# RWKV-7 chunk stage of a two-layer decoder step: the second eight heads' 16-token level moved into the first half of a chunk

## The chip, the core and the metric

The kernel runs on one core of a Trainium2 chip. A core has five engines that run their own instruction streams and meet at semaphores: TensorE (PE, matrix products; PEld is its weight load), VectorE (DVE), ScalarE (ACT), GpSimd (POOL) and SyncE (SP), which issues most DMAs. The metric is the device time of one execution in microseconds (us); the median of 3 runs before the change is 3222.52 us (3216.25 to 3230.39).

## The reference

Two layers over a prompt (1024 tokens and 16 meta tokens) and eight samples of 4 tokens: layer 0 mixes tokens with latent attention, layer 1 with RWKV-7 time mixing; each is followed by a squared-ReLU MLP. The change lies in RWKV-7's recurrence, cut here to what it computes for each of 16 heads of 64 channels:

```python
def _wkv_step(S, inp):
    r, w, k, v, a, b = inp
    sa = jnp.einsum('bhvk,bhk->bhv', S, a)
    S = S * w[:, :, None, :] + sa[..., None] * b[:, :, None, :] + v[..., None] * k[:, :, None, :]
    return S, jnp.einsum('bhvk,bhk->bhv', S, r)

S_T, y = lax.scan(_wkv_step, wkv0, (tm(r), tm(decay), tm(k), tm(v), tm(-kk), tm(kk * a)))
```

Here r, k, v are projections of the token-shifted input, decay = exp(-exp(log_w)), kk the normed key and a a learned rate. y then goes through a group norm over each head, gets a bonus term, is multiplied with a gate g and projected.

## The kernel before

The recurrence is computed in chunks of 128 tokens: chunks 0 to 7 for the prompt, and a tail of 48 tokens (the last 16 tokens of the prompt and the samples). Within a chunk, sa of all tokens is the solution of a triangular system, (1 + M) sa = first sums, where M holds the products of decayed keys with b-keys below the diagonal. The kernel builds the inverse of the 128x128 triangle of each head level by level. VectorE makes the inverses of the 16x16 blocks on the diagonal (`low_inverses`, L4047), for the next chunk, at the end of each chunk. From them TensorE makes the larger ones: level 16 joins pairs of 16-blocks to 32-blocks, level 32 to 64-blocks, level 64 to the full 128. Each level is two products with a copy between: the *crossed* product of M with the smaller inverses, which VectorE (level 16, L4038, with a mask) or ScalarE (levels 32 and 64) copies negated out of PSUM, and the *joined* product, which gives the new off-diagonal block. ScalarE prepares the operand of a crossed product by spreading blocks: `spread_16` (L3062, 2 instructions of L3054) fills X4 from XE, `spread_32` (L3069) fills X5 (2 of L3054) and the diagonal of XT (4 of L3048) from what VectorE's `blocks_32` (L4041: add L4043, transpose L4045) made of level 16's result. Level 64 (L1529) first transposes blocks (L693), which ScalarE copies to XW6 (`take_turned`), then does its two products; the copies between are `take_w_64` (L3092) and `take_x_64` (L3096).

The sixteen heads are worked on in two halves of eight, d = 0 and d = 1. A half runs: masks of the products of keys (VectorE, L4007), level 16, 32, 64, `first_sums`, `finals` (sa, the state's product, the output's product). Between these steps the same loops prepare chunk c + 1 and finish chunk c - 1: `rates`, `decays` (L2997 to L3001), running sums (L3953), `a_keys` and `b_keys` (decayed keys on VectorE, L3936 and L3989), `key_factors` (ScalarE, eight instructions, L3103), `before_half` (TensorE's products of b-keys with the decayed keys, the M of the next chunk, masked by VectorE, L4007), `diagonals` (ScalarE, L3011, what `low_inverses` reads), and for the chunk before its centring, norm (POOL, L2375 to L2379), gates (TensorE) and their product (VectorE, L4140).

What sets the order: the code is written once for each engine (`chunk` appears in the streams of TensorE, ScalarE, VectorE and GpSimd), and each engine runs it strictly as written. PSUM is used as two rings of four banks, `ra` (drained by ScalarE) and `rv` (drained by VectorE): a product waits until the bank's last content was copied out, and the copies take the banks in the order in which TensorE filled them. `keep_busy` (L1440) is an empty product of 128x256, whose result nobody reads.

Of the kernel before, what the change touches and what calls it, by code (L numbers as in the profile page):

```python
# [216 lines left out]
def program(nc, A, O):  # L217
    ctx = ExitStack()
    with ctx:
# [457 lines left out]
        def _(pe):  # L677
# [815 lines left out]

            def level_16(c, d, ma, filler):

                apart(x4_b.sem, c * x4_b.per + d + 1)
                b = narrow(rv, rv.filled.n - 3)
                for j in range(8):
                    for rows, cols in diagonal(8 * d + j):
                        ins = mm(b[rows, j * 64:(j + 1) * 64], ma[rows, cols], X4[rows, j * 64:(j + 1) * 64], True, True)  # L1500
                rv.done(ins)
                w4_at = rv.filled.n
                filler()
                if d == 1:
                    keep_busy(rv)
                b = narrow(rv, w4_at)
                for j in range(8):
                    h = 8 * d + j
                    for rows, _ in diagonal(h):
                        ins = mm(b[rows, j * 32:(j + 1) * 32], W4[rows, j * 64:(j + 1) * 64], XD[rows, h * 32:(h + 1) * 32], True, True)  # L1510
                rv.done(ins)
# [19 lines left out]
            def level_64(d, ma, fillers):  # L1531

                crossed_at = ra.filled.n
                fillers[2]()
                keep_busy(ra)
                b = narrow(ra, crossed_at)
                for j in range(8):
                    ins = turn(b[0:64, j * 64:(j + 1) * 64], XT[0:64, j * P:j * P + 64], 64)
                ra.done(ins)
                turned_at = ra.filled.n  # L1540
                fillers[0]()
                keep_busy(ra)
                b = narrow(ra, turned_at)
                for j in range(8):
                    h = 8 * d + j
                    ins = mm(b[64:P, j * 64:(j + 1) * 64], ma[0:64, h * P + 64:(h + 1) * P], XW6[0:64, j * 64:(j + 1) * 64], True, True)
                ra.done(ins)
                w6_at = ra.filled.n
                fillers[1]()
                b = narrow(ra, w6_at)  # L1550
                for j in range(8):
                    ins = mm(b[0:64, j * 64:(j + 1) * 64], XW6[64:P, j * 64:(j + 1) * 64], XT[64:P, j * P + 64:(j + 1) * P], True, True)
                ra.done(ins)

            def chunk(c, par, nth, finish=True, prepare=True, wn=P):
# [14 lines left out]

                def finals(d, taken, stated):

                    keep_busy(ra)
                    ra.wait_drained()
# [37 lines left out]
                k_with_both(0, 1, ar)  # L1612
                level_16(c, 0, ma, lambda: turn_b_k(c, P))
                bonus_sums(c, P)
# [4 lines left out]
                v_in[par].wait(pe, nth)  # L1619
                level_64(0, ma, [when(prepare, lambda: key_sums(c + 1, wn)), lambda: first_sums(0), nothing])  # L1620
                finals(0, when(prepare, lambda: rates(c + 1, wn, 0)), when(prepare, lambda: (rates(c + 1, wn, 1), key_scales(c + 1, wn))))

                b_with_r(1, ar)
                k_with_both(1, 0, ar)
                k_with_both(1, 1, ar)
                level_16(c, 1, ma, nothing)
                if finish:
# [10 lines left out]

                level_32(c, 1, ma, when(prepare, lambda: before(0)))
                level_64(1, ma, [nothing, lambda: first_sums(1), when(prepare, lambda: before(1))])  # L1640
                finals(1, when(finish, lambda: turn_z(c - 1, P, Y[1 - par])), nothing)

# [810 lines left out]
        def _(act):  # L2453
# [608 lines left out]
            def spread_16(c, d):  # L3062

                low_b.wait(act, c)
                if not isinstance(c, int) or c > 0 or d > 0:
                    e32_b.wait(act, c, d)
                signal(pair_blocks(X4, XE[:, d * 256:(d + 1) * 256]), x4_b)
# [63 lines left out]
            def chunk(c, par, finish=True, prepare=True, wn=P):  # L3131
                if prepare:
                    lora_columns(c + 1, wn)
                tokens(P)
                bonus_out(P)
                spread_32(c, 0)
# [16 lines left out]
                if prepare:  # L3153
                    both_rates(c + 1, wn)
                spread_16(c, 1)
                if prepare:
                    decays(c + 1, wn, wn == TAIL)
                take(Y[par][:, 0:512], P, 512)
                if wn == TAIL:
                    decays_before(c + 1, wn)  # L3160
                if prepare:
                    key_factors(c + 1, wn)

                spread_32(c, 1)
                take_w_32()
                take_x_32()
                take_turned()
# [125 lines left out]
        def _(dve):  # L3293
# [868 lines left out]
            def chunk(c, par, finish=True, prepare=True, wn=P):  # L4162
# [14 lines left out]
                if finish:  # L4177
                    centre(c - 1, P, Y[1 - par])
                if prepare:
                    clamp(c + 1, wn)  # L4180
# [4 lines left out]
                if finish:  # L4185
                    scale_outputs(c - 1, P, Y[1 - par])
                new_taken()
                new_summed(0)
# [6 lines left out]
                k_with_both(1)  # L4195
                level_16(1)
                if prepare:
                    a_keys(c + 1, 1 - par, wn)
                blocks_32(c, 1)
                if prepare:  # L4200
                    b_keys(c + 1, wn)
# [197 lines left out]
```

## Time and profile before

| what | value |
|---|---|
| median of 3 runs | 3222.52 us |
| profiled execution | 3217.26 us, of them 3215.5 us span |
| granted TensorE clock, mean | 0.991 |
| busy, share of the span | PE 96%, PEld 89%, DVE 58%, ACT 42%, POOL 39% |
| chunk stage | chunk 0 starts at 1800.45 us, the tail's first products at 2330.65 us |
| chunk 3 (2002.83 to 2069.30, 66.47 us), busy us | PE 61.17, DVE 51.06, ACT 39.05, POOL 18.34, clock 1.00 |
| chunk 7 | crossed product of level 16, second half, starts at 2304.86 us; its eight key factors take 2.64 us |

How to read it: a row of a timeline gives the start in us from the span's start, the length in us, engine, line, operation, what it writes and reads with their shapes, and in brackets how long the engine sat idle before it and which instruction ended the wait. Most tiles are pieces of one allocation, `arena`; so an instruction is best known by its line and shape. The timeline shows two records for each of the small products, so 16 products read x32. A product's length includes the end of the pipeline: the next may start some 0.07 us before it ends. PEclk is the granted clock as a share of 2.4 GHz.

### The profile page before, as it was taken

The page shows a single profiled execution, that of the slowest core. Times are in us where ns is not written, and L with a number is a line of the kernel's source. Part 1 is how long each engine was busy: PE and PEld are TensorE (multiplying, and loading weights), DVE is VectorE, ACT ScalarE, POOL GpSimd, SP SyncE. Part 2 cuts the span into 40 slices and gives each one's busy share as a digit, 9 for nine tenths or more (in the row PEclk, how much of TensorE's full clock was granted, in tenths as well). Part 3 has the DMA queues.
Part 4 walks back from the last instruction along what each step waited for, and adds up shares of the span by engine and source line. Part 5 has one row for each costly group of instructions (what it writes and reads, how often), then busy time and mean ns, then how long its engine had stood idle before and what let it go on. Part 6 is the DMA issues. An engine that isn't in the chain of part 4 may idle for free.

```text
span 3215.5 us, 70230 instructions
## 1 busy us (share of the span) xinstructions
PE 3085.3 (96%) x25828; PEld 2853.0 (89%) x25828; DVE 1880.4 (58%) x3193; ACT 1358.9 (42%) x2823; POOL 1261.7 (39%) x877
## 2 busy tenths in 40 slices
PE   8999999998999999999999999998999999999998
PEld 8788887798999999998899878787888899999998
DVE  5666663257444578864412577777735644457885
ACT  4344445424554433322223455656522455443332
POOL 0000000025766777732222122232224467677771
PEclk9999999999999999999999999999999999999999
DMA  3222225402544544431123201001151254554442
GB/s 116 61 79 74 74 60 179 151 13 80 160 158 158 176 148 144 138 103 56 61 81 117 75 21 47 28 28 34 42 174 37 84 161 153 158 175 148 148 134 78
DMA packets 307311, 330.49 MB, mean 103 GB/s; under 512 B 54366, under 2 KB 289809, under 8 KB 306994
## 3 DMA queue, kind: packets, MB, share of 16 engines
q1 hardware_dynamic: 301166, 308.54, 30.3%
q0 software_dynamic: 5904, 19.21, 1.9%
q8 instruction: 133, 2.18, 0.3%
q14 instruction: 56, 0.46, 0.0%
q10 hardware_dynamic: 52, 0.10, 0.0%
HBM read 232.05 MB, written 116.16 MB: 108 GB/s over the span
## 4 chain that ended last, share of the span: by engine, by line
PE 74%; DVE 10%; PEld 5%; POOL 3%; ACT 3%; issue 2%; DMA 1%; PEldq 0%; DVEq 0%; SPq 0%; ACTq 0%; POOLq 0%
PE bank L685 70%; PEld bank L685 5%; PE bank L693 4%; DVE arena L3936 1%; DVE hT L4007 1%; POOL wloA L2215 1%; POOL arena L2215 1%; DVE arena L3600 1%; DVE x_mix L3890 1%; POOL wloS L2215 1%; DMA arena<-in_mla_w_qkv_a 1%; DVE arena L3311 1%; DVE arena L3471 1%; DVE arena L3953 0%; DVE x_lo L3897 0%
## 5 line engine op out<-in xcount | busy, mean ns | idle before, releaser
L685 PE MATMUL bank<-arena 64*128 64x128 f32 (+19 forms) x6718 | 770.7, 303 | 33.9 <-DVE hT L4007 12.9
L685 PEld LDWEIGHTS bank<-arena 128*128 128x128 f32 (+9 forms) x6718 | 602.5, 162 | 168.2 <-issue 35.1
L2462 ACT COPY arena<-bank 128x512 f32<-128x512 f32 (+14 forms) x518 | 230.6, 485 | 590.7 <-PE bank L685 390.0
L2741 ACT ACTIVATE whiS<-arena 128x512 fp32r<-128x512 f32 x180 | 112.9, 627 | 405.4 <-POOL arena L2215 392.1
L2215 POOL TENSOR_TENSOR wloA<-arena,whiA 128x512 fp32r<-128x512 f32 x180 | 263.5, 1478 | 14.0 <-ACT whiA L2735 14.0
L2215 POOL TENSOR_TENSOR wloS<-arena,whiS 128x512 fp32r<-128x512 f32 x180 | 241.1, 1353 | 49.1 <-ACT whiS L2741 49.1
L2215 POOL TENSOR_TENSOR arena<-arena 128x512 f32<-128x512 f32 x120 | 165.5, 1380 | 230.9 <-PE bank L685 230.9
L3805 DVE TENSOR_TENSOR hT<-hT,bank 128x536 f32<-128x536 f32 x280 | 197.4, 706 | 83.2 <-PE bank L685 82.9
L693 PE MATMUL bank<-table,arena 128*128 128x128 f32 (+5 forms) x1422 | 181.1, 269 | 28.2 <-DVE arena L3483 13.0
L3620 DVE TENSOR_TENSOR arena<-std,bank 128x268 f32<-128x268 f32 x192 | 80.4, 431 | 216.0 <-PE bank L685 208.2
L685 PE MATMUL bank<-hiT,whiS 128*128 128x268 f32 x768 | 199.9, 289 | 6.9 <-DVE fb L3615 3.5
L693 PEld LDWEIGHTS bank<-table,arena 128*128 128x128 f32 (+5 forms) x1422 | 146.2, 135 | 54.2 <-issue 40.7
L2185 POOL TENSOR_TENSOR arena<-arena 128x536 f32<-128x536 f32 (+3 forms) x18 | 39.2, 2177 | 330.2 <-ACT arena L2711 299.8
L3746 DVE TENSOR_TENSOR arena<-arena 128x268 f32<-128x268 f32 x224 | 140.7, 668 | 42.2 <-ACT arena L2779 39.9
L685 PEld LDWEIGHTS bank<-hiT,whiS 128*128 128x128 f32 x768 | 146.3, 191 | 8.0 <-DVE fb L3615 4.1
L3323 DVE TENSOR_TENSOR hT<-hT,bank 128x268 f32<-128x268 f32 (+2 forms) x120 | 55.1, 468 | 156.1 <-PE bank L685 155.7
L3890 DVE SCALAR_TENSOR_TENSOR x_mix<-arena,prm 128x384 f32<-128x384 f32 (+1 forms) x96 | 57.8, 674 | 149.5 <-PEq L1280 149.2
L685 PE MATMUL bank<-hi,whiA 128*128 128x268 f32 x512 | 132.6, 288 | 2.6 <-DVE fb L3615 1.7
L2208 POOL TENSOR_TENSOR q<-arena,q 64x1072 fp32r<-64x1072 f32 x4 | 9.8, 2459 | 316.4 <-ACT q L2603 316.4
L685 PE MATMUL bank<-loT,whiS 128*128 128x268 f32 x512 | 132.7, 288 | 0.0
L685 PE MATMUL bank<-fb,whiS 128*128 128x268 f32 x512 | 132.3, 288 | 0.0
L685 PE MATMUL bank<-fb,whiA 128*128 128x268 f32 x512 | 131.9, 287 | 0.0
(356 smaller groups left out, 8980.2 us busy)
## 6 DMA issues: line engine op xcount, KB each, us to landing
u_scratch<-arena SPq DMA_DIRECT2D x480, 134.0 KB, 1.8
arena<-in_ffn_w_up SPq DMA_DIRECT2D x64, 512.0 KB, 4.1
arena<-u_scratch SPq DMA_DIRECT2D x56, 536.0 KB, 5.1
arena<-in_ffn_w_down SPq DMA_DIRECT2D x112, 256.0 KB, 3.8
arena<-u_scratch SPq DMA_DIRECT2D x56, 402.0 KB, 5.8
arena<-past_scratch SPq DMA_DIRECT2D x32, 640.0 KB, 6.9
past_scratch<-in_cache_kv_latent SPq DMA_DIRECT2D x128, 128.0 KB, 2.4
past_scratch<-in_cache_k_rope SPq DMA_DIRECT2D x128, 32.0 KB, 2.1
```

What stands on the lines that cost most here:

```text
L685: return pe.matmul(out, lhsT, rhs, start=first, stop=last, skip_group_check=group)
L693: return pe.transpose(out, src, ident[0:rows, 0:rows])
L2185: lane.do(pool.tensor_tensor(sq[:, 0:n, :], sq[:, 0:n, :], sq[:, n:2 * n, :], ALU.add))
L2215: return pool.tensor_tensor(out, a, b, op)
L2462: lane.do(act.copy(dst, b if view is None else view(b)), ring.drained)
L2741: ins = act.activation(hi[name][:, :, :], src, ACT.Copy)
L3311: ins = dve.scalar_tensor_tensor(out=dst[:, k, at:at + w], in0=src[:, k, at:at + w], scalar=prm[:, k, row:row + 1], in1=by, op0=ALU.mult, ...
L3323: lane.do(dve.tensor_tensor(hT[:, k, at:at + w], hT[:, k, at:at + w], b[:, 0:w], ALU.add), ring.drained)
L3620: dve.tensor_tensor(out, to, (BV, BA)[s][CHAIN[i]][:, 0:TS], ALU.add).then_inc(to_dve_b[layer].sem, 1)
L3746: dve.tensor_tensor(f.us[q, s], f.us[a, s], f.us[b, s], op).then_inc(diff_b[layer].sem, 1)
L3805: ins = dve.tensor_tensor(to[i], to[i], made, ALU.add)
L3890: ins = dve.scalar_tensor_tensor(out=x_mix[:, k, at:at + w], in0=DX[:, k, at:at + w], scalar=prm[:, k, R_MU + row:R_MU + row + 1], in1=nT[ ...
```

## The change

The crossed product of level 16 of the second eight heads moves from the second half to the first, where it stands for an empty product before the transposes of level 64; the joined product stands for the empty product before `finals`. With them move VectorE's mask, the add and transpose of the 32-blocks, and ScalarE's `spread_16`, now ahead of the bonus copy. ScalarE's `spread_32` of the second half is put where `spread_16` stood, ahead of `decays`; the two copies of level 32 go ahead of `key_factors`. In the second half the products with the decayed keys of the next chunk (`before`) move from level 32 and level 64 into level 64 alone, in the place of two empty products. Per chunk five empty products go.

```diff
-            def level_16(c, d, ma, filler):
+            def crossed_16(c, d, ma):
...
-                w4_at = rv.filled.n
-                filler()
-                if d == 1:
-                    keep_busy(rv)
-                b = narrow(rv, w4_at)
+                mark["crossed_16", c, d] = rv.filled.n
+
+            def joined_16(c, d):
+
+                b = narrow(rv, mark["crossed_16", c, d])
...
                 crossed_at = ra.filled.n
                 fillers[2]()
-                keep_busy(ra)
                 b = narrow(ra, crossed_at)
...
                 fillers[0]()
-                keep_busy(ra)
+                if d == 0:
+                    keep_busy(ra)
...
-                def finals(d, taken, stated):
-
-                    keep_busy(ra)
+                def finals(d, hidden, taken, stated):
+
+                    hidden()
...
-                level_16(c, 0, ma, lambda: turn_b_k(c, P))
+                crossed_16(c, 0, ma)
+                turn_b_k(c, P)
+                joined_16(c, 0)
...
-                level_64(0, ma, [when(prepare, lambda: key_sums(c + 1, wn)), lambda: first_sums(0), nothing])
-                finals(0, when(prepare, lambda: rates(c + 1, wn, 0)), when(prepare, lambda: (rates(c + 1, wn, 1), key_scales(c + 1, wn))))
+                level_64(0, ma, [when(prepare, lambda: key_sums(c + 1, wn)), lambda: first_sums(0), lambda: crossed_16(c, 1, ma)])
+                finals(0, lambda: joined_16(c, 1), when(prepare, lambda: rates(c + 1, wn, 0)),
+                       when(prepare, lambda: (rates(c + 1, wn, 1), key_scales(c + 1, wn))))
...
-                level_16(c, 1, ma, nothing)
...
-                level_32(c, 1, ma, when(prepare, lambda: before(0)))
-                level_64(1, ma, [nothing, lambda: first_sums(1), when(prepare, lambda: before(1))])
-                finals(1, when(finish, lambda: turn_z(c - 1, P, Y[1 - par])), nothing)
+                level_32(c, 1, ma, nothing)
+                level_64(1, ma, [when(prepare, lambda: before(1)), lambda: first_sums(1), when(prepare, lambda: before(0))])
+                finals(1, lambda: keep_busy(ra), when(finish, lambda: turn_z(c - 1, P, Y[1 - par])), nothing)
```

ScalarE and VectorE (`spread_16` now waits for the mask after the crossed product that last read X4):

```diff
                 tokens(P)
+                spread_16(c, 1)
                 bonus_out(P)
                 spread_32(c, 0)
...
-                spread_16(c, 1)
+                spread_32(c, 1)
                 if prepare:
                     decays(c + 1, wn, wn == TAIL)
                 take(Y[par][:, 0:512], P, 512)
...
+                take_w_32()
+                take_x_32()
                 if prepare:
                     key_factors(c + 1, wn)
-
-                spread_32(c, 1)
-                take_w_32()
-                take_x_32()
                 take_turned()
...
                     centre(c - 1, P, Y[1 - par])
+                level_16(1)
...
                     scale_outputs(c - 1, P, Y[1 - par])
+                xt_b.wait(dve, c, 1)
+                blocks_32(c, 1)
                 new_taken()
...
-                level_16(1)
                 if prepare:
                     a_keys(c + 1, 1 - par, wn)
-                blocks_32(c, 1)
```

**TensorE, second half of chunk 3, before.** `64x64 x16` is a crossed product, `64x32 x16` level 16's joined product, `table 128x256` an empty product, `128x512` and `128x256 x2` the gates, `128x128 x8` a half of the products with the next chunk's decayed keys; the order counts each product once.

```order
L685 MATMUL bank<-arena,hT 64x64 x16
L685 MATMUL bank<-table 128x256
L685 MATMUL bank<-arena,hT 64x32 x16
L685 MATMUL bank<-arena 128x512
L685 MATMUL bank<-arena 128x256 x2
L685 MATMUL bank<-hT 64x64 x16
L685 MATMUL bank<-arena 128x128 x8
L685 MATMUL bank<-table 128x256
L685 MATMUL bank<-arena,hT 64x64 x16
L685 MATMUL bank<-arena 128x128 x8
L685 MATMUL bank<-table 128x256
L693 MATMUL bank<-table,arena 64x64 x8
```

The same place of the changed kernel:

```order
L685 MATMUL bank<-arena 128x256 x8
L685 MATMUL bank<-arena 128x512
L685 MATMUL bank<-arena 128x256 x2
L685 MATMUL bank<-hT 64x64 x16
L685 MATMUL bank<-table 128x256
L685 MATMUL bank<-arena,hT 64x64 x16
L685 MATMUL bank<-arena 128x128 x8
L693 MATMUL bank<-table,arena 64x64 x8
L685 MATMUL bank<-arena 128x128 x8
L685 MATMUL bank<-arena,hT 64x64 x8
L685 MATMUL bank<-arena 128x128 x4
```

The first rows (level 16 and an empty product) are gone, the gates follow the keys' products (`128x256 x8`) at once, and both halves of the decayed keys' products stand around the transposes (L693).

**ScalarE, the same half, before,** from `spread_16` (L3054 arena) on; L2997 to L3001 are the decays, L3103 the key factors, L3054 hT with L3048 `spread_32`, L3078 and L3084 the copies of level 32, `64x512` the copy of the transposed blocks.

```order
L3054 ACTIVATE arena<-arena,table 128x8x32 x2
L2997 ACT_TABLE_LOAD
L2997 ACTIVATE arena<-arena 128x1024
L2999 ACTIVATE arena<-arena 128x8
L3000 ACTIVATE arena<-arena 128x8
L3001 ACTIVATE arena<-arena 128x1024
L2462 COPY arena<-bank 128x512
L3103 ACTIVATE arena<-arena,prm 128x128 x8
L3054 ACTIVATE hT<-arena,table 128x8x32 x2
L3048 COPY arena<-arena 32x8x32 x4
L3078 ACTIVATE hT<-bank 32x8x32 x2
L3084 COPY arena<-bank 32x8x32 x2
```

And of the changed kernel, whose lines stand 2 to 4 further down:

```order
L3056 ACTIVATE hT<-arena,table 128x8x32 x2
L3050 COPY arena<-arena 32x8x32 x4
L2999 ACT_TABLE_LOAD
L2999 ACTIVATE arena<-arena 128x1024
L3001 ACTIVATE arena<-arena 128x8
L3002 ACTIVATE arena<-arena 128x8
L3003 ACTIVATE arena<-arena 128x1024
L2464 COPY arena<-bank 128x512
L3082 ACTIVATE hT<-bank 32x8x32 x2
L3088 COPY arena<-bank 32x8x32 x2
L3107 ACTIVATE arena<-arena,prm 128x128 x8
L2464 COPY arena<-bank 64x512
```

`spread_32` now stands ahead of the decays, and the key factors between the second copy of level 32 and the copy of the transposed blocks.

**VectorE, end of the first half of the changed kernel:** L4124 is the centring, L4041 the mask of level 16, L4046 and L4048 the add and transpose of the 32-blocks, L4154 the state update.

```order
L4124 TENSOR_TENSOR arena<-arena 128x1024
L4041 TENSOR_TENSOR hT<-bank,arena 128x512
L3943 TENSOR_SCALAR arena<-bank 128x128
L4128 TENSOR_REDUCE arena<-arena 128x16
L3965 RECIPROCAL arena<-arena 128x128
L4133 RECIPROCAL arena<-arena 128x16
L4135 TENSOR_TENSOR arena<-arena 128x1024
L4046 TENSOR_TENSOR arena<-arena,bank 128x256
L4048 STREAM_TRANSPOSE arena<-arena 128x256
L4154 TENSOR_TENSOR arena<-bank,table 128x512
L3939 TENSOR_TENSOR arena<-arena 128x512 x2
```

In the kernel before, L4041, L4046 and L4048 (there L4038, L4043 and L4045) are not in this piece; they stand in the second half around the decayed keys (L3936).

## Rows read from the trace of the kernel before

**Rows 1.** Timeline of TensorE, chunk 3: start, length, line, tiles, [idle before].
```profile
2012.07 1.15 PE L685 MATMUL bank<-hT 64*64 64x64 f32 x32 [1.09 <-ACT hT L3054]
...
2016.30 0.60 PE L693 MATMUL bank<-table,arena 64*64 64x64 f32 x8 [0.29 <-ACT arena L3084]
...
2023.12 0.70 PE L685 MATMUL bank<-table 128*128 128x256 f32 x2
...
2041.79 1.12 PE L685 MATMUL bank<-arena,hT 64*64 64x32 f32 x32 [0.36 <-DVE hT L4038]
2042.84 1.99 PE L685 MATMUL bank<-arena 128*128 128x512 f32 x6
2045.22 1.15 PE L685 MATMUL bank<-hT 64*64 64x64 f32 x32 [0.39 <-ACT hT L3054]
2047.38 1.16 PE L685 MATMUL bank<-arena 64*128 64x128 f32 x16 [1.01 <-DVE arena L4140]
...
2053.29 1.11 PE L685 MATMUL bank<-arena,hT 64*64 64x64 f32 x16
...
2057.16 1.14 PE L685 MATMUL bank<-arena 64*64 64x64 f32 x16
```

**Rows 2.** Timeline of VectorE, chunks 2 and 3.
```profile
1989.30 1.06 DVE L4059 STREAM_TRANSPOSE arena<-arena 128x512 f32<-128x512 f32 x1 [0.49 <-ACTq L3013]
...
2002.83 3.80 DVE L4007 TENSOR_TENSOR hT<-bank,arena 128x512 f32<-128x512 f32 x6 [1.09 <-PE bank L685]
...
2029.69 2.79 DVE L3936 TENSOR_TENSOR arena<-arena 128x512 f32<-128x512 f32 x2
...
2040.96 0.68 DVE L4038 TENSOR_TENSOR hT<-bank,arena 128x512 f32<-128x512 f32 x1
2041.75 1.43 DVE L3936 TENSOR_TENSOR arena<-arena 128x1016 f32<-128x1016 f32 x2
...
2044.08 1.22 DVE L3936 TENSOR_TENSOR arena<-arena 128x1024 f32<-128x1024 f32 x1
...
2051.37 1.29 DVE L4007 TENSOR_TENSOR arena<-bank,arena 128x512 f32<-128x512 f32 x2 [1.54 <-PE bank L685]
...
2055.77 1.05 DVE L4059 STREAM_TRANSPOSE arena<-arena 128x512 f32<-128x512 f32 x1 [0.49 <-ACTq L3013]
```

**Rows 3.** Timeline of ScalarE, chunk 3.
```profile
2009.98 0.27 ACT L2462 COPY arena<-bank 128x128 f32<-128x128 f32 x1 [0.91 <-PE bank L685]
2010.86 0.91 ACT L3054 ACTIVATE hT<-arena,table 128x256 f32<-128x256 f32 x2 [0.61 <-DVE arena L4045]
...
2032.62 0.91 ACT L3054 ACTIVATE arena<-arena,table 128x256 f32<-128x256 f32 x2 [0.17 <-issue]
...
2037.37 1.06 ACT L2997 ACTIVATE arena<-arena 128x1024 f32<-128x1024 f32 x1 [2.55 <-DVE arena L3957]
...
2039.95 3.19 ACT L3103 ACTIVATE arena<-arena,prm 128x128 f32<-128x128 f32 x8
...
2044.83 1.63 ACT L3048 COPY arena<-arena 32x256 f32<-32x256 f32 x4
...
2052.57 0.58 ACT L2462 COPY arena<-bank 64x512 f32<-64x512 f32 x1 [1.54 <-PE bank L693]
2053.17 2.55 ACT L3011 ACTIVATE arena<-arena 32x512 f32<-32x512 f32 x4
```

**Rows 4.** Timeline of GpSimd, chunk 3.
```profile
2028.84 2.36 POOL L2379 TENSOR_TENSOR arena<-arena 128x1024 f32<-128x1024 f32 x1
...
2039.65 2.37 POOL L2351 TENSOR_TENSOR arena<-arena 128x1024 f32<-128x1024 f32 x1 [8.45 <-ACT arena L3001]
```

**Rows 5.** Timeline of TensorE, chunk 7.
```profile
2315.89 1.11 PE L685 MATMUL bank<-arena,hT 64*64 64x64 f32 x16
```

**Rows 6.** TensorE in chunk 0.
```profile
1810.86 0.64 PE L685 MATMUL bank<-arena 128*32 128x128 f32 x16 [2.09 <-ACT arena L2462]
```

**Rows 7.** Windows, chunk 0: length, busy PE, PEld, DVE, ACT, POOL; PEclk, DMA, GB/s.
```profile
1812.00:1814.00 2.00, 1.54 (x13) 0.84 (x13) 0.00 (x0) 1.98 (x7) 0.00 (x0) 0.50 1.00 354
```

More of the change, by code:

```diff
@@ L3064, in spread_16 @@
                 low_b.wait(act, c)
-                if not isinstance(c, int) or c > 0 or d > 0:
-                    e32_b.wait(act, c, d)
+                if d == 1:
+                    act.wait_ge(v_drained, mark["crossed_16", c, 0])
+                elif c > 0:
+                    act.wait_ge(v_drained, mark["crossed_16", c - 1, 1])
                 signal(pair_blocks(X4, XE[:, d * 256:(d + 1) * 256]), x4_b)
@@ L4195, in chunk @@
                 k_with_both(1)
-                level_16(1)
                 if prepare:
                     a_keys(c + 1, 1 - par, wn)
-                blocks_32(c, 1)
-                if prepare:
                     b_keys(c + 1, wn)
```

## The prediction

> **What bounds the kernel now.** I went from the page to the windows view, then read one chunk of the stage engine by engine in the timelines. The page has TensorE busy for 96% of the span, so a gain must come from TensorE's waits or from work taken off it. The changed code runs only in the eight chunks of the mixing stage (1800 to 2333 us of 3215.5). A steady chunk repeats every 66.47 us (2055.77 less 1989.30, [rows 2]); TensorE is busy for 61.2 of it at full clock (table above). Its 5.3 us of waits lie where four 16-to-64-token levels follow one another. In the second half the order reads: crossed product of level 16, which ends at 2040.7, an empty product, a wait of 0.36 us for VectorE, joined product, gates, a wait of 0.39 for ScalarE's spread, crossed product of level 32, a wait of 1.01 until VectorE has made the keys of the next chunk, and only at 2053.29 the first product of the last level [rows 1]. From there TensorE runs without a wait to the end of the chunk, so what the change does to that start, and to the third product of the level (2057.16), is what it does to the chunk. VectorE is the next candidate: at the chunk's start it waits 1.09 us for TensorE [rows 2], and by no more than that may it fall behind TensorE.
>
> I number times as in chunk 3, whose first mask starts at 2002.83.
>
> **First half: what is added.** ScalarE spreads the second eight heads' blocks ahead of the bonus copy: 0.91 us and 0.17 of issue (2032.62, [rows 3]). Ahead of the bonus copy and of spread_32 it idles 0.91 and 0.61 us [rows 3]; 1.08 fits into 1.52, so spread_32 still starts at 2010.86. The crossed product (1.15 us) takes the place of an empty one (0.63 to 0.70) before the transposes at 2016.30, where TensorE waits 0.29 for ScalarE anyway [rows 1]; it ends at 2016.4, 0.1 late. The next two steps wait for ScalarE's copies, which swallow that. VectorE's mask for it (0.68) falls into an idle stretch. The joined product (1.12, of which 1.05 until the next may start) takes the place of the empty one of 0.70 at 2023.12, where nothing waits: TensorE is 0.35 us late from there on. VectorE's add and transpose come then, and it has nothing else until the state's product at 2029.
>
> Is 0.35 us paid? VectorE's state update starts at 2029.69 and its two adds take 2.79 us, where the same two take 1.42 elsewhere; GpSimd's add runs from 2028.84 to 2031.20 [rows 2, 4]. I read the 1.37 us as VectorE standing still until GpSimd is done. Its end does not move with 0.35 us, so VectorE's chain to the masks at 2037.26 and their end at 2040.96 stay where they are. Price in a steady chunk: 0. Bounds: 0 and 0.35.
>
> The Trainium skill has this as a rule ("SBUF — State Buffer", section "Who interferes with whom"): a VectorE instruction with two SBUF inputs and a GpSimd instruction that reads SBUF use one read interface, and the second to issue blocks until the first is done. The trace agrees (1.37 us).
>
> **Second half: what goes.** TensorE has both products of level 16 behind it. After the keys' masks the gates can start where the crossed product stood, at 2041.79 - 0.36 - 0.70 - 1.08 = 2039.65; they take 2.0 us (the banks they need are drained by the third to fifth of the six masks, in time), so level 32's crossed product starts at 2041.65 and no longer at 2045.22. ScalarE has spread its operand long before: spread_32 now stands where the 0.91 us of spread_16 stood, and is longer by its four copies, 1.63 us. Behind it ScalarE waits 2.55 us for the running sums of the decays (2037.37, [rows 3]); that cover takes all of it in a steady chunk, with 0.9 left.
>
> From the crossed product to ScalarE's last copy of level 32 it takes 2016.30 - 0.14 - 2012.07 = 4.09 us in the first half [rows 1], so here until 2045.75. And now the edit that costs: the eight key factors (3.19 us, 2039.95, [rows 3]) ran in ScalarE's gap before level 32; they now stand between it and the copy of the transposed blocks. ScalarE is done with them at 2048.95, copies until 2049.55 (0.58), and TensorE's first product of the last level starts at 2049.7: 3.6 us earlier than 2053.29.
>
> Meanwhile VectorE: masks end at 2040.96, the level-16 mask (0.68) is gone. The decayed keys can be issued at 2041.05. But GpSimd's product runs from 2039.65 to 2042.02 [rows 4], and both read two SBUF tiles: by what 2029.69 showed the keys wait, and end at 2043.2, where they end now (2041.75 + 1.43). The add and transpose of level 32 are gone too, so b_keys start at 2043.2 where they started at 2044.08: 0.9 earlier. The product with the decayed keys follows b_keys' start by 2047.38 - 2044.08 = 3.3 us, so it starts at 2046.5. TensorE has waited from 2044.8, 1.7 us, its longest wait of the chunk. Then 1.1 of product, 0.55 of transposes, the second product at 2048.15, done at 2049.3; the masks of it 2049.35 to 2050.65 (1.29, [rows 2]); ScalarE's diagonals 2.55 us to 2053.25; only behind them its copy for the third product, 0.6, so that product starts at 2054.05. By TensorE's own pace (2057.16 - 2053.29 = 3.87) it would be 2053.55. The later counts: 2057.16 - 2054.05 = **3.1 us a steady chunk**.
>
> VectorE's inverses start with the diagonals at 2053.3 and not at 2055.77: 2.45 earlier, TensorE 3.1. The 0.65 us between them fit into VectorE's 1.09 [rows 2].
>
> **The sum.** Chunks 1 to 6: 6 x 3.1 = 18.6. Chunk 0: TensorE waits for ScalarE there (2.09 us at 1810.86, [rows 6]), so the 1.08 us of spread_16 are paid, and without an earlier chunk's output GpSimd has no add that hides the 0.35: 3.1 - 1.4 = 1.7, of which I take 1.6, since spread_32 has less cover there. Chunk 7: its crossed product started at 2304.86; the gates take that place, 0.35 late, and the first product of the last level follows at 2305.2 + 2.0 + 4.1 + 2.64 (shorter key factors) + 0.7 = 2314.7, against 2315.89 [rows 5]: 1.2. In all **21.4 us**. The profiled execution took 3217.3 us, so it would be 3195.9; the median of the runs is 3222.5, 5 us higher, and that is what I start from: 3222.5 - 21.4 = **3201 us**. Everything behind the stage hangs on it in a chain and moves with it.
>
> **Bounds.** Of what no row shows: the keys blocked by GpSimd (end 2043.2) or not (2042.4); the longest wait of TensorE (1.7 us) without a price or with one; the 0.35 us. Per steady chunk that makes 3.6 at best, 1.2 at worst; I take 3.1, since the one row that shows such an overlap (2029.69) shows the full block.
>
> **Rivals.**
> *VectorE sets the end.* If its inverses begin later than I say, or its slack of 1.09 is less than it looks, TensorE waits at the next chunk's first masks and the gain is VectorE's, 2.45: 6 x 2.45 + 2.8 = 17.5, 3205 us. For it: just 0.45 us of slack would be left. Against: each step of it was read from rows.
> *No block of the keys.* They end 0.8 earlier, everything behind b_keys too, and TensorE's own pace and the key factors decide: 3.6, so 6 x 3.6 + 2.8 = 24.4, 3198 us. For it: the rows cannot show who would wait. By the page's rule above the block comes, since GpSimd starts first.
> *The clock falls once a chunk.* Five empty products of 0.63 us go, and a wait of 1.7 us comes. In chunk 0, after a wait of 2.09 us, the granted clock was 0.50, which is 1.2 GHz, from 1812 to 1814 [rows 6, 7], and it was back at full only near 1816. Some 3.8 us at half speed cost up to 1.9 us; in seven chunks 13, so 3222.5 - 21.4 + 13 = 3214 us. Against: waits of 1.0 to 1.1 us, three a chunk, leave the clock at 1.00 now.
> *Slower: the clock stays down.* The same mechanism, longer: from 2049.7 TensorE works without a pause, and each microsecond of it at 1.2 GHz costs half. From 6.2 us at half speed a chunk (3.1 / 0.5) the gain is gone; 12 us cost 6.0 - 3.1 = 2.9 a chunk, 20 in seven: 3243 us. Against: in chunk 0 the clock was back after dense work.
>
> **Chances.** Forecast 0.52 (3196 to 3207 by itself), VectorE 0.15, no block 0.12, clock once a chunk 0.17, clock for long 0.04. A change of this kernel can be told from none from about 0.5%, 16 us. Below 3206 lie nearly all of the first and third and over half of the second: faster 0.70; within 0.5% 0.26; slower 0.04. Range 3193 to 3214.
>
> **What would show it.** The period of the diagonals' transpose on VectorE should be 63.4 us (66.47 before). TensorE's wait ahead of the decayed keys' product should be 1.7 us, and the keys on VectorE 2.1 us from issue where GpSimd overlaps. ScalarE should have no idle time between the last copy of level 32, the key factors and the copy of the transposed blocks. VectorE's wait at a chunk's first mask should shrink from 1.09 to about 0.45; at 0 with TensorE waiting there, the first rival holds. A granted clock below 1.00 in chunks 1 to 7 speaks for the third. A period above 65 us would make the forecast wrong.

## The result

The changed kernel takes 3229.16 us (median of 20 runs, 3218.71 to 3240.49) where the kernel before takes 3222.84 us (20 runs, 3215.61 to 3230.39): the ratio is 1.0025, 95% interval 1.0015 to 1.0034. It is slower by a quarter of a percent; 3201 was forecast. Its profiled execution took 3219.73 us, one of its shorter ones: the profile below shows some 9 us less of the loss than the median run has.

The page of the profile after, its first lines and the clock:

```profile
span 3217.9 us, 70070 instructions
PE 3077.1 (96%) x25748; PEld 2861.2 (89%) x25748; DVE 1889.7 (59%) x3193; ACT 1359.4 (42%) x2823; POOL 1263.1 (39%) x877
...
PEclk9999999999999999999999989999889999999999
```

With five empty products a chunk gone, TensorE is busy for 57.2 us in a chunk with full clock and no longer for 61.2. Over the whole kernel its busy time fell by 8 us only: the rest went into products that took longer. The mean granted clock fell from 0.991 to 0.983, and three slices of the chunk stage and the tail (the 24th, 29th and 30th of 40) show an eight where there were nines.

The windows view of the changed kernel, four stretches: columns as in the rows of before, with the busy us of each engine and PEclk third from the end.

```profile
core 0: us, PE busy (x) PEld busy (x) DVE busy (x) ACT busy (x) POOL busy (x), PEclk, DMA share, GB/s
1998.58:2061.76 63.18, 57.22 (x749) 50.45 (x749) 52.47 (x88) 39.06 (x85) 18.33 (x9) 1.00 0.10 35
1919.00:1937.00 18.00, 18.00 (x114) 17.18 (x111) 16.19 (x41) 7.35 (x14) 0.00 (x0) 0.53 0.09 30
2308.00:2326.00 18.00, 16.27 (x89) 15.71 (x90) 12.82 (x38) 6.03 (x13) 1.86 (x3) 0.53 0.42 79
2346.00:2364.00 18.00, 18.00 (x253) 15.20 (x250) 3.85 (x7) 2.01 (x4) 8.89 (x4) 0.53 0.40 139
```

Two kinds of chunk show. The first row is a chunk from one diagonals' transpose to the next with the clock at 1.00: it takes 63.18 us, where before it took 66.47 [rows 2]. The second row is the last level of chunk 1: TensorE has no wait at all and a clock of 0.53, that is nearly all of it at the lower of the two levels, 1.2 GHz. I call such a stretch at 1.2 GHz a spell. Read in steps of one microsecond from 1780 to 2380 us, the spells of the changed kernel add up to 65 us: 3.4 and 3.4 in chunk 0, 3.4 and 17.1 in chunk 1, 3.4 in chunk 2, 17.1 in chunk 7 and 17.1 in the tail. Those of the kernel before add up to 17 (3.4 in chunk 0 and 13.7 in the tail). The difference of 48 us at half speed is 24 us of time. The forecast's gain of 21.4 less those 24 leaves a loss of 2.6, and the two spans differ by 2.4.

The table gives the periods of VectorE's transpose that opens `low_inverses`, from the one for chunk n to the one for chunk n + 1 (each is made at the end of the chunk ahead of its own, so the spell from 1919 to 1937 lies in both the second and the third column):

| kernel | 0 to 1 | 1 to 2 | 2 to 3 | 3 to 4 | 4 to 5 | 5 to 6 | 6 to 7 | 7 to tail |
|---|---|---|---|---|---|---|---|---|
| before | 71.18 | 66.47 | 66.46 | 66.47 | 66.47 | 66.47 | 66.46 | 61.71 |
| after | 69.70 | 69.30 | 73.33 | 63.18 | 63.19 | 63.17 | 63.18 | 59.29 |

From the first to the last of them after is 7.4 us shorter (524.3 against 531.7); behind the last, where chunk 7's last level and the tail each ran some 18 us at 0.53, it is 8.7 longer, and ahead of the first 1.1. That makes the 2.4 us by which the spans differ.

TensorE in a chunk with full clock (chunk 3 of the changed kernel), second half:

```profile
2047.25 3.05 PE L685 MATMUL bank<-arena 64*128 64x256 f32 x14 [1.11 <-DVE hT L4010]
...
2052.34 1.15 PE L685 MATMUL bank<-arena,hT 64*64 64x64 f32 x32 [0.33 <-ACT hT L3082]
2055.23 1.16 PE L685 MATMUL bank<-arena 64*128 64x128 f32 x16 [1.74 <-DVE arena L4143]
...
2058.22 1.11 PE L685 MATMUL bank<-arena,hT 64*64 64x64 f32 x16 [0.48 <-ACT arena L2464]
...
2062.54 1.11 PE L685 MATMUL bank<-arena 64*64 64x64 f32 x16 [0.38 <-ACT arena L3096]
```

The wait ahead of the product with the decayed keys is 1.74 us where it was 1.01 [rows 1], the last level starts at 2058.22, 0.48 us after TensorE was ready, and its third product waits 0.38. The wait of 1.74 us alone does not always bring a fall: in this execution it stands in chunks 2 to 6 and the clock stayed at 1.00 behind it each time. The falls came behind waits of 1.60 (chunk 0), 2.09 (chunk 1) and 2.19 us (chunk 7), and in the first halves of chunks 0 to 2 behind 1.67 to 4.27 us. And the same place in chunk 1, where the clock fell:

```profile
1917.97 1.16 PE L685 MATMUL bank<-arena 64*128 64x128 f32 x16 [2.09 <-DVE arena L4143]
...
1919.38 1.86 PE L685 MATMUL bank<-arena 64*128 64x128 f32 x15
1921.17 1.96 PE L685 MATMUL bank<-arena,hT 64*64 64x64 f32 x16
1923.07 2.07 PE L685 MATMUL bank<-arena 128*128 128x128 f32 x8
1924.93 3.51 PE L685 MATMUL bank<-std,hT 128*128 128x64 f32 x16
1928.38 1.97 PE L685 MATMUL bank<-arena 64*64 64x64 f32 x16
```

Here the wait was 2.09 us, and from 1919 on each product takes nearly twice its length: 1.96 for 1.11, 2.07 for 1.16, 3.51 for 1.90. That lasts until 1937, through work without a gap.

The other engines in the chunk with full clock, VectorE, then ScalarE, then GpSimd:

```profile
2011.49 3.80 DVE L4010 TENSOR_TENSOR hT<-bank,arena 128x512 f32<-128x512 f32 x6 [0.46 <-PE bank L685]
...
2049.81 3.34 DVE L3939 TENSOR_TENSOR arena<-arena 128x1016 f32<-128x1016 f32 x3
```

```profile
2046.03 1.06 ACT L2999 ACTIVATE arena<-arena 128x1024 f32<-128x1024 f32 x1 [1.06 <-DVE arena L3960]
...
2054.28 3.19 ACT L3107 ACTIVATE arena<-arena,prm 128x128 f32<-128x128 f32 x8
2057.50 0.58 ACT L2464 COPY arena<-bank 64x512 f32<-64x512 f32 x1
2059.15 2.55 ACT L3013 ACTIVATE arena<-arena 32x512 f32<-32x512 f32 x4 [1.07 <-DVEq L4017]
```

```profile
2048.31 2.36 POOL L2353 TENSOR_TENSOR arena<-arena 128x1024 f32<-128x1024 f32 x1 [8.45 <-ACT arena L3003]
```

VectorE's first wait is 0.46 us (1.09 before, [rows 2]); its three key instructions take 3.34 us, where the same three take 2.63 when GpSimd is out of the way (below); ScalarE had 1.06 us of cover left ahead of the decays (0.9 forecast) and runs from the key factors into the copy of the transposed blocks without a gap.

### The profile page after: what moved, and what is told of

Its sections match the earlier page's. It is cut to its first block, busy times and chain, and to the rows that moved or that the text cites. A ratio compares the mean times of both kernels' runs of the same rounds, so it can differ in the third digit from the quotient of the medians.

```text
span 3217.9 us, 70070 instructions
## 1 busy us (share of the span) xinstructions
PE 3077.1 (96%) x25748; PEld 2861.2 (89%) x25748; DVE 1889.7 (59%) x3193; ACT 1359.4 (42%) x2823; POOL 1263.1 (39%) x877
## 4 chain that ended last, share of the span: by engine, by line
PE 75%; DVE 10%; PEld 5%; ACT 3%; POOL 2%; issue 1%; DMA 1%; DVEq 1%; PEldq 0%; SPq 0%; ACTq 0%; POOLq 0%
PE bank L685 71%; PEld bank L685 5%; PE bank L693 4%; DVE arena L3939 1%; DVE hT L4010 1%; POOL wloA L2217 1%; DVE arena L3603 1%; POOL arena L2217 1%; POOL wloS L2217 1%; DVE x_mix L3893 1%; DMA arena<-in_mla_w_qkv_a 1%; DVE arena L3314 1%; DVE arena L3474 1%; DVE arena L3956 0%; DVE x_lo L3900 0%
## 5 line engine op out<-in xcount | busy, mean ns | idle before, releaser
L685 PE MATMUL bank<-arena 64*128 64x128 f32 (+19 forms) x6718 | 781.3, 306 | 42.5 <-DVE hT L4010 12.8
L685 PEld LDWEIGHTS bank<-arena 128*128 128x128 f32 (+9 forms) x6718 | 614.6, 165 | 173.0 <-issue 39.9
L693 PE MATMUL bank<-table,arena 128*128 128x128 f32 (+5 forms) x1422 | 183.7, 271 | 26.3 <-DVE arena L3486 13.1
L693 PEld LDWEIGHTS bank<-table,arena 128*128 128x128 f32 (+5 forms) x1422 | 148.6, 136 | 48.2 <-issue 33.8
L685 PE MATMUL bank<-arena,hT 64*64 64x64 f32 (+2 forms) x1920 | 126.6, 239 | 7.2 <-ACT hT L3082 3.5
L685 PEld LDWEIGHTS bank<-arena,hT 64*64 64x64 f32 (+1 forms) x1920 | 116.1, 155 | 18.7 <-issue 18.7
```

Source lines behind the costliest of these rows:

```text
L685: return pe.matmul(out, lhsT, rhs, start=first, stop=last, skip_group_check=group)
L693: return pe.transpose(out, src, ident[0:rows, 0:rows])
```

## The experiments

Each was run 4 to 12 times, beside the kernel before, whose median was then 3219.4 to 3220.6 us. The places are named by the second half of a chunk: the first place is the wait ahead of the product with the decayed keys, the second the wait ahead of the last level's first product.

**Is it the waits?** Two empty products into the 1.74 us wait:

```diff
-                level_64(1, ma, [when(prepare, lambda: before(1)), lambda: first_sums(1), when(prepare, lambda: before(0))])
+                level_64(1, ma, [when(prepare, lambda: before(1)), lambda: first_sums(1), when(prepare, lambda: ([keep_busy(ra) for _ in range(2)], before(0)))])
```

> The changed kernel with two empty products (2 x 0.63 us) put into its wait of 1.74 us ahead of the product with the decayed keys. Theory (the lost time is TensorE's clock, which falls in that wait and keeps the last level at half speed): steady chunks keep their 63.2 us, the clock stays at 1.00 in chunks 1 to 6, no spell at half speed begins at that place; time 3199 us (0.993 of before). Rival A (the spells begin somewhere else, the wait only happens to be near): spells as in the changed kernel, time 3225 to 3235. Rival B (the empty products themselves cost): period 63.2 + 1.3 = 64.5, time near 3210. In chunk 0 and chunk 7 the wait ahead of the last level (1.6 and 2.2 us) is left, so a spell there may remain.

Measured: 0.9952 of the kernel before (0.9935 to 0.997), 3209.7 us, with spells at half speed in chunks 0, 1, 2 and 7 in the profiled execution (its slowest, 3221.8) and a period of 63.16 to 63.6 in the others. Half-way: right in kind, but 10 us short of the theory's 3199. The clock fell in chunks 1 and 2 as well, where the theory had none: in chunk 1 from 1928 on, behind the last level's third product and its wait of 0.73 us, in chunk 2 in the first half, behind a wait of 2.69.

The same with one more empty product after the second product with the decayed keys (`lambda: (before(1), keep_busy(ra))`):

> As the run before, with one more empty product between the second product with the decayed keys and the last level's first product (a wait of 0.48 us in steady chunks, 1.6 in chunk 0, 2.2 in chunk 7). Theory: no spell of half speed in any chunk except perhaps the first half of chunk 0; period 63.2 to 63.3 us, because the third product of the last level is released by ScalarE's diagonals, not by this; time 3197 us. Rival A: no better than the changed kernel, 3225 to 3235. Rival B: 0.1 to 0.2 us more per chunk than the run before.

Measured: **0.9934** (0.9918 to 0.995), 3200.2 us, runs within 3198.6 to 3204.3. TensorE in this kernel, chunk 3:

```profile
2038.49 1.13 PE L685 MATMUL bank<-table 128*128 128x256 f32 x4
2040.31 1.16 PE L685 MATMUL bank<-arena 64*128 64x128 f32 x16 [0.69 <-DVE arena L4143]
```

```profile
2042.76 0.70 PE L685 MATMUL bank<-table 128*128 128x256 f32 x2
2043.38 1.14 PE L685 MATMUL bank<-arena,hT 64*64 64x64 f32 x16
```

The two empty products fill 1.13 us, the wait left is 0.69; the third stands where 0.48 us of wait was. The period is 63.2 us (64.0 and 63.5 in two chunks), and no spell at half speed is left ahead of the tail's. TensorE does more work than in the changed kernel (58.86 us busy in a chunk, 57.22 there) and the kernel is 29 us faster. This is the forecast's 3201 us; the theory had 3197.

**Count or place?** Three empty products a chunk as well, but ahead of `finals` of the second half, where TensorE does not wait (`lambda: keep_busy(ra)` becomes `lambda: [keep_busy(ra) for _ in range(4)]`):

> The changed kernel with three more empty products a chunk, as many as in the run with both places filled (0.9934 of before), but put where TensorE has no wait, ahead of finals of the second half. Theory (what counts is that the waits of the last level are filled): the clock falls as in the changed kernel, and 3 x 0.63 = 1.9 us a chunk are paid on top: period about 65.1 where the clock is full, 3235 to 3250 us. Rival (any empties hold the clock up, wherever they stand): clock at 1.00 in chunks 1 to 6, 3210 to 3215 us.

Measured: 1.0069 (1.0053 to 1.0084), 3238.8 us, half speed in chunks 0, 1, 2, 5, 6 and 7 (0.51 at 1988 to 1995, for one). Where the clock was full the period was 64.14 us, not 65.1: four empty products in a row take 1.99 us where one takes 0.70, so three more add 1.3 and not 1.9. The place decides.

**Order or empties?** The kernel before, in its own order, without the five empty products:

```diff
                 fillers[2]()
-                keep_busy(ra)
...
                 fillers[0]()
-                keep_busy(ra)
+                if d == 0:
+                    keep_busy(ra)
```

(and without the one in `level_16` for d = 1 and the one of `finals` for d = 0).

> The kernel before, in its own order, without the five empty products per chunk that the change took out. Theory: its waits become longer but stay below 1.7 us, so that spells at half speed are fewer than in the changed kernel or none; if the empties alone held the clock up, spells appear in chunks 1 to 7 here as well and the time is 3230 to 3245. If the reordering is what brings the fall (one wait of 1.74 us instead of three short ones), the time is 3218 to 3223, 0 to 0.5 us a chunk less than before, with the clock at 1.00 in chunks 1 to 6.

Measured: 1.0059 (1.0036 to 1.0081), 3240.2 us. Windows of this kernel around the last level of a first half (level 64 of the first eight heads, chunk 3), then one period of it:

```profile
core 0: us, PE busy (x) PEld busy (x) DVE busy (x) ACT busy (x) POOL busy (x), PEclk, DMA share, GB/s
2018.00:2023.00 5.00, 4.33 (x47) 4.13 (x45) 2.29 (x3) 3.17 (x6) 0.72 (x1) 1.00 0.01 3
2023.00:2031.00 8.00, 8.00 (x55) 7.43 (x56) 0.77 (x2) 4.05 (x10) 6.32 (x3) 0.57 0.00 0
1919.78:1987.91 68.13, 61.05 (x750) 53.67 (x748) 50.79 (x88) 39.02 (x85) 18.33 (x9) 0.95 0.10 32
```

The clock falls in chunk after chunk (0.57 from 2023 to 2031; 0.95 over a period, which is 68.13 and not 66.47 us long), and from chunk 1 to chunk 7 no wait of TensorE is longer than 1.2 us. But these falls lie in the *first* half, in chunks 1, 2, 3, 4, 6 and 7 (one more, of 3.4 us, begins in chunk 7's second half). TensorE in chunk 3, its first half and then its second:

```profile
2010.36 1.15 PE L685 MATMUL bank<-hT 64*64 64x64 f32 x32 [1.10 <-ACT hT L3053]
...
2014.54 0.60 PE L693 MATMUL bank<-table,arena 64*64 64x64 f32 x8 [0.87 <-issue]
...
2022.15 5.02 PE L685 MATMUL bank<-arena 128*128 128x64 f32 x34 [0.67 <-ACT arena L3095]
```

```profile
2042.61 1.12 PE L685 MATMUL bank<-arena,hT 64*64 64x32 f32 x32 [0.99 <-DVE hT L4037]
...
2048.08 1.16 PE L685 MATMUL bank<-arena 64*128 64x128 f32 x16 [1.01 <-DVE arena L4139]
...
2053.24 1.11 PE L685 MATMUL bank<-arena,hT 64*64 64x64 f32 x16 [0.76 <-ACT arena L2461]
```

In the first half the two waits of 0.87 and 0.67 us stand where the empty products were. The changed kernel has level 16's moved products in these two places, and behind them no fall begins in any chunk of its profile. In the second half three empty products are gone as well and the waits are 0.99, 1.01 and 0.76 us, and in the profiled execution no spell begins there in chunks 1 to 6. So two things follow. A long wait is not needed for a fall, and taking the empties out of the old order costs 20 us. But where the changed kernel loses its clock, in the second half, the removal alone did not bring the fall in this execution; what the new order adds there is the longer wait.

**One empty product, in one place or the other.** Only in the first (`range(1)`), only in the second:

> The changed kernel with one empty product, not two, in the first place and none in the second; 1.1 us of the wait of 1.74 are left. Theory: between the changed kernel and the run with two in the first place (0.9952 of before): 3210 to 3225 us. Rival (a single empty product is enough): 3200 to 3210 us.

> The changed kernel with one empty product in the second place alone (ahead of the last level's first product; waits of 0.48, 1.6 and 2.2 us in chunks 3, 0 and 7). Theory: the wait of 1.74 us is left, so the clock still falls in some chunks, less often than in the changed kernel: 3208 to 3225 us. Rival (the second wait alone is the cause): as good as with both places filled, 3198 to 3203 us.

Measured: 0.9988 (0.9977 to 1.0), 3216.9 us, runs from 3203 to 3222; and 0.9979 (0.9963 to 0.9996), 3213.2 us, runs from 3203 to 3239. Both lie where the theory had them. A profile alone would mislead: the one of the first shows no spell in chunks 1 to 6 (its execution took 3206), and six of its ten other runs took over 10 us more.

**Key factors early.** ScalarE's `key_factors` back ahead of `take_w_32()`:

> The changed kernel with ScalarE's eight key factors (3.19 us) put back ahead of its two copies of level 32. Theory: the last level's first product starts earlier (right behind the transposes' copy, some 0.5 us sooner), but its third product is released by the diagonals and stays: period 63.2 us, unchanged; the wait ahead of the last level goes (0.48, 1.6 and 2.2 us in chunks 3, 0 and 7), the wait of 1.74 us stays, so spells at half speed remain in some chunks but not in chunk 7: 3215 to 3230 us. Rival (key factors in the last level are what costs): period 62.7 or less and a time below 3205.

Measured: 1.0087 (1.0066 to 1.0107), 3249.6 us: 20 us above the theory's range. TensorE around one last level:

```profile
2118.10 1.15 PE L685 MATMUL bank<-arena,hT 64*64 64x64 f32 x32 [0.71 <-ACT hT L3082]
2120.62 1.16 PE L685 MATMUL bank<-arena 64*128 64x128 f32 x16 [1.36 <-DVE arena L4143]
```

```profile
2127.92 1.11 PE L685 MATMUL bank<-arena 64*64 64x64 f32 x16 [0.90 <-ACT arena L3096]
2128.97 0.95 PE L685 MATMUL bank<-table 128*128 128x256 f32 x2
2129.71 3.67 PE L685 MATMUL bank<-arena 128*128 128x64 f32 x16
2133.17 1.91 PE L693 MATMUL bank<-table,arena 128*128 128x128 f32 x8
```

The wait ahead of the last level's first product is gone, as expected. The other waits are 0.71, 1.36 and 0.90 us; in the changed kernel they were 0.33, 1.74, 0.48 and 0.38. So the longest is shorter, the last one, ahead of the third product, is longer, and the sum is the same (3.0 and 2.9 us). The clock falls around this place in each of the chunks 1 to 6, where the changed kernel's profile shows it in one of them. Chunk 7 has no spell in its last level, as expected. The spell brings a second one, in the next first half. VectorE, then GpSimd, then TensorE there:

```profile
2148.98 2.94 DVE L4003 TENSOR_TENSOR arena<-arena 128x1024 f32<-128x1024 f32 x1
```

```profile
2148.92 1.93 POOL L2348 TENSOR_TENSOR arena<-arena,prm 128x1024 f32<-128x1024 f32 x1 [5.47 <-DMA arena<-k_scratch]
```

```profile
2153.98 1.97 PE L685 MATMUL bank<-hT 64*64 64x64 f32 x32 [2.82 <-ACT hT L3056]
...
2157.14 3.36 PE L685 MATMUL bank<-arena,hT 64*64 64x64 f32 x64
```

Half speed held TensorE back, but not VectorE's inverses nor GpSimd, which so comes to its product (2148.92) just when VectorE scales the state: 2.94 us instead of 1.22. Behind it TensorE waits 2.82 us for the operand of level 32, and is slow again (1.97 for 1.15). The changed kernel has it too: waits of 2.69 and 4.27 us at 1882.02 and 1956.42, after the spells of chunks 0 and 1.

**Does that clash matter?** GpSimd's next keys only after the state is scaled (`s_b.wait(pool, c)` ahead of `scale_keys`):

> The changed kernel, in which GpSimd starts on the next chunk's keys only when VectorE has scaled the state. Theory (a spell at half speed in the last level holds TensorE back but not VectorE and GpSimd; in the next first half GpSimd's product then falls on VectorE's state update, and TensorE waits 2.7 to 4.3 us for the level-32 operand and slows again): the wait ahead of level 32 in the first half stays at 1.1 us in every chunk and no spell begins there; the first falls, in the wait of 1.74 us, stay: 3212 to 3226 us, below the changed kernel. Rival (the spells in the first half have nothing to do with GpSimd): waits of over 2.5 us ahead of level 32 remain, 3226 to 3236 us.

Measured: 1.0023 (1.0004 to 1.0042), 3229.2 us, the changed kernel's own time and above the theory's 3212 to 3226. The mechanism is as said: from chunk 1 on the wait ahead of level 32 is 1.1 us and no spell begins there. But the gain did not come. In the profiled execution (3247.4 us) the clock fell around the last level of nearly every chunk, with spells of up to 20.5 us. The clash follows from a spell; taking it away alone does not shorten the median.

**GpSimd's block of the decayed keys.** GpSimd's product of r after the b-keys (`b_b.wait(pool, c)` for `dec_b.wait(pool, c)` in `decay_r`):

> The changed kernel, in which GpSimd makes its product of r with the decays (2.36 us, now beside VectorE's decayed keys) only after VectorE's b-keys. Theory: VectorE's first decayed-keys instruction no longer stands 0.8 us behind GpSimd, the wait of 1.74 us ahead of the decayed keys' product becomes 0.9 to 1.0, period 62.8 to 63.2; with the shorter wait the clock falls in fewer chunks: 3200 to 3215 us. Rival (VectorE was not blocked by GpSimd there, the wait is VectorE's own work): wait 1.74, period 63.2, time 3225 to 3235 as the changed kernel.

Measured: 0.9984 (0.9974 to 0.9995), 3216.6 us, just above the theory's 3200 to 3215. VectorE, GpSimd and TensorE:

```profile
2050.11 2.63 DVE L3939 TENSOR_TENSOR arena<-arena 128x1016 f32<-128x1016 f32 x3
```

```profile
2054.15 2.37 POOL L2353 TENSOR_TENSOR arena<-arena 128x1024 f32<-128x1024 f32 x1 [13.98 <-DVE arena L3992]
```

```profile
2054.82 1.16 PE L685 MATMUL bank<-arena 64*128 64x128 f32 x16 [1.03 <-DVE arena L4143]
...
2058.52 1.11 PE L685 MATMUL bank<-arena,hT 64*64 64x64 f32 x16 [1.19 <-ACT arena L2464]
```

The three key instructions take 2.63 us, 0.71 less than in the changed kernel, and the wait is 1.03. The block is shown. Yet the wait ahead of the last level grew from 0.48 to 1.19, since the key factors did not move, and the clock still falls in the last level: 1850 to 1872 and 1987 to 2001 in the profiled execution.

**All of it.** Late product of GpSimd, one empty product in each place, with the key factors early and late:

> GpSimd's product late, ScalarE's key factors ahead of the copies of level 32, and one empty product in each of the two places of the last level. Theory: with the first wait shorter and filled, the last level is released by the diagonals 0.7 us earlier: period 62.5 to 62.8, clock 1.00 in chunks 1 to 6, time 3193 to 3197 us. Rival (early key factors are harmful by themselves, as their run at 1.0087 of before could be read): time above 3215.

> As the run before but with the key factors where the changed kernel has them. Theory: first product of the last level still behind the key factors, third product at TensorE's own pace: period 62.9, clock 1.00 in chunks 1 to 6, 3196 to 3199 us. The difference to the run before is the price of the key factors in the last level, 0.1 to 0.4 us a chunk.

Measured: early **0.9913** (0.9898 to 0.9927), 3193.5 us, period 62.44; late 0.9929 (0.9917 to 0.9942), 3196.1 us, period 62.7. The first has the lowest median of all, 27 us below the kernel before; the intervals of the two overlap, but its period is shorter by 0.28 us, within the 0.1 to 0.4 expected. TensorE in it:

```profile
2036.97 1.15 PE L685 MATMUL bank<-arena,hT 64*64 64x64 f32 x32 [0.71 <-ACT hT L3082]
2038.05 0.70 PE L685 MATMUL bank<-table 128*128 128x256 f32 x2
2038.76 1.16 PE L685 MATMUL bank<-arena 64*128 64x128 f32 x16
```

Behind the empty product no wait is left. So early key factors, the worst version without fillers, do no harm with fillers and a late product of GpSimd. Fillers with early key factors but without the late product were not run.

## Why the prediction was wrong

*The order of the work: right.* A steady chunk was to take 63.4 us and takes 63.18; the wait ahead of the decayed keys was to be 1.7 us and is 1.74; VectorE's slack was to shrink to 0.45 and is 0.46. The last level's third product comes 3.3 us earlier in the chunk, not 3.1. The first half costs nothing in steady chunks, as said: the first product of the second half starts 35.76 us behind the chunk's first mask in both kernels. Chunk 0 was to give 1.6 us and its period is 1.5 shorter. GpSimd's block of the decayed keys, 0.8 us by the estimate, is 0.71 by the run that takes it away, so the rival without the block was wrong; and VectorE kept 0.46 us of slack, so the rival in which it sets the end was wrong too. With three empty products put back the kernel takes 3200.2 us, the forecast.

*The step that failed: "the longest wait of TensorE (1.7 us) without a price or with one", taken without, and with it the count of the five empty products as work that only stood in waits.* They were priced at nothing because their time was idle time; what they kept up, the clock, had no term in the sum. Three of them put back into the waits of the last level bring 3200.2 us, three put where TensorE does not wait 3238.8. The rival "the clock falls once a chunk" was the right mechanism with too small a size: it took one short spell, 3.8 us at half speed, 1.9 us paid, from chunk 0 [rows 7]. Two of the three spells in the changed kernel's last levels are 17.1 us long (1919 to 1937, 2308 to 2326), 8.5 us paid for each. From the product with the decayed keys in chunk 1 (1917.97) to the one in chunk 2 (1992.06) it takes 74.1 us, with full clock 63.2: 10.9 us for one such spell and the clash behind it. Two of them eat the forecast's 21.4 us. The rival's bill was 13 us; the profiled execution paid 24, and the median run took 9 us more.

*The argument against that rival was weak as well.* "Waits of 1.0 to 1.1 us leave the clock at 1.00 now" was read from a kernel with five more empty products a chunk than the changed one has. In the first half of the kernel before without them the clock falls with waits of 1.10, 0.87 and 0.67 us. In its second half it did not fall in chunks 1 to 6 with 0.99, 1.01 and 0.76; but there the change also brings a wait of 1.7 us, of which the row said nothing.

*The range* took the worst steady chunk at 1.2 us of gain; a chunk with a spell loses 3 to 7 us against before. The changed kernel's runs spread over 22 us (before over 15), and the slow ones have the lower clock: the mean granted clock was 0.977 in the longest (3240.49 us) and 0.983 in the shortest (3218.71). So the clock falls more often in some runs than in others. What decides that is open; only the places where it can happen were shown.

## What to carry to other kernels

An instruction whose result nobody reads may hold up TensorE's clock: before it is removed or its wait made longer, price the dense work *behind* it at half speed, not the gap itself. Rearrange and fill in one step: the same order was 1.0025 of before with open waits and 0.9934 with three empty products in them, and a reordering that was harmful without fillers (1.0087) was part of the fastest version (0.9913, which also has GpSimd's product late). Judge such a change by the spread of many runs and by the clock read microsecond by microsecond, since one profile may have caught a run in which nothing fell.

## What the runs showed of the hardware

A spell at 1.2 GHz does not end with the wait that opened it. In the changed kernel TensorE was busy for 18.00 of 18.00 us from 1919 to 1937 and the clock was 0.53; in the version with GpSimd waiting for the state there is a stretch of 22 us of unbroken work with this clock:

```profile
1922.00:1944.00 22.00, 22.00 (x141) 21.18 (x138) 16.69 (x43) 8.02 (x15) 2.57 (x2) 0.53 0.13 40
```

In the same place with a filled wait, the same products run at 1.00 throughout. Short spells of 3.4 and 6.8 us stand beside those of 13.7, 17.1 and 20.5 us; which one comes was not settled here. In the tail, whose products are 8 and 32 columns wide, both kernels have such a spell with no wait over 0.4 us in the 6 us ahead of it (13.7 us before, 17.1 after in the profiled executions).

And a plain copy can be caught by GpSimd as well: VectorE's copy of eight columns (L4002) took 1.75 us at 1951.48 instead of 0.17 and ended at 1953.23, where GpSimd's product, begun at 1950.86, ended at 1953.20; at 1877.07 it took 1.76 us in the same way.
